# Linear attention's level stage with one mixed array of queries and keys, a fourth product bank, and a reordered start, in a four-layer network on one core

## The reference, cut to what matters

```python
def first_block(...):        # layers 0 and 1
    for i in range(2):
        u = modulate(h, shift, scale)
        y = attention_mixer(u) if i == 0 else ssm_mixer(u)
        h = layer_norm(ALPHA * h + g_m * y, ...)
        f = squared_relu_mlp(modulate(h, ...), ff_w1[i], ff_w2[i])   # 1024 -> 4096 -> 1024
        h = layer_norm(ALPHA * h + g_f * f, ...)

def second_block(...):       # layers 2 and 3
    for i in range(2):
        a = rms_norm(h) * (1 + scale) + shift
        o = even_mix(a) if i == 0 else attention(a)
        h = h + gate * o
        h = h + gate2 * conv_ffn(rms_norm(h) * (1 + scale2) + shift2)
    return rms_norm(h_lat, g_norm_final)

def even_mix(h, ...):        # layer 2: Fourier mixing beside gated linear attention
    u_f, q, k, v, r, z = split(h @ w_in)
    loga = log_sigmoid(z @ w_gate + b_gate) / 16       # a decay per key channel and token
    o = gla_scan(q, k, v, loga forwards) + flip(gla_scan(flipped))
    # within a chunk: A[i, j] = sum_c q[i,c] k[j,c] exp(sum of loga between j and i),  j <= i
```

## Time and profile before

| | |
|---|---|
| device time, median of 3 runs | 4260.65 us (4259.33 to 4261.77) |
| profiled execution | 4259.32 us, span 4257.5 us |
| busy in the span | PE 4039.0 us (95%), DVE 1786.7 (42%), ACT 815.5 (19%), POOL 240.6 (6%) |
| mean granted clock | 0.980 of full |
| first 28 us | DMA busy share 0.96, 359 GB/s |
| level stage, 2573.6 to 2769.5 us | 195.90 us: PE 141.57 busy, DVE 150.75, ACT 71.11, POOL 0.00; granted clock 0.78 |
| pairs of layer 2, 2896.2 to 3273.7 us | 377.50 us: PE 371.00 busy, DVE 278.43 |
| pairs of layer 3, 3824.5 to 4098.2 us | 273.70 us: PE 264.90 busy, DVE 220.83 |

### The profile page before, as it was taken

One profiled execution on the slowest core, in us unless ns is written; L12 is line 12 of the kernel. 1 busy time (PEld: TensorE's weight loads), 2 busy tenths in 40 slices (PEclk: granted clock), 3 DMA queues, 4 the chain that ended last, 5 costly groups with the idle time before them and its releaser, 6 DMA issues.

```text
span 4257.5 us, 45853 instructions
## 1 busy us (share of the span) xinstructions
PE 4039.0 (95%) x18528; PEld 2498.0 (59%) x18528; DVE 1786.7 (42%) x3040; ACT 815.5 (19%) x1549; POOL 240.6 (6%) x228
## 2 busy tenths in 40 slices
PE   7999999999999999999999996799999999999999
PEld 5676588744455555558646545645555444758864
DVE  0254523100266655444102028736776015437841
ACT  1265111100112321111102022321100021531000
POOL 1000000000013441300000000000000000000000
PEclk9999999999999999999999997799999999999999
DMA  4255011211112211322223012301111112002222
GB/s 179 90 198 180 20 60 60 70 59 43 41 68 101 90 65 64 120 73 84 95 74 113 35 42 100 139 21 60 54 56 60 54 66 70 2 21 89 80 89 74
DMA packets 201230, 325.82 MB, mean 77 GB/s; under 512 B 4274, under 2 KB 90616, under 8 KB 200896
## 3 DMA queue, kind: packets, MB, share of 16 engines
q1 hardware_dynamic: 195136, 302.00, 20.6%
q0 software_dynamic: 5888, 20.91, 1.5%
HBM read 320.74 MB, written 2.16 MB: 76 GB/s over the span
## 4 chain that ended last, share of the span: by engine, by line
PE 88%; DVE 7%; ACT 3%; issue 1%; DMA 1%; POOL 0%; DVEq 0%; ACTq 0%; SPq 0%
PE PS L973 27%; PE PS L1013 22%; PE PS L948 3%; PE PS L1485 3%; PE PS L926 3%; PE PS L1064 3%; PE PS L1499 3%; PE PS L885 2%; PE PS L805 2%; PE PS L1486 1%; PE PS L1646 1%; PE PS L1178 1%; PE PS L1656 1%; PE PS L1337 1%; PE PS L1147 1%
## 5 line engine op out<-in xcount | busy, mean ns | idle before, releaser
L973 PE MATMUL PS<-RING,BIG 128*128 128x512 f32 x2352 | 1016.9, 593 | 3.7 <-DVEq L1713 1.6
L973 PEld LDWEIGHTS PS<-RING,BIG 128*128 128x128 f32 x2352 | 445.5, 190 | 557.1 <-issue 552.2
L1013 PE MATMUL PS<-UT,RING 128*128 128x256 f32 (+1 forms) x2432 | 648.2, 414 | 35.1 <-ACT BIG L2510 18.3
L1013 PEld LDWEIGHTS PS<-UT,RING 128*128 128x128 f32 x2432 | 461.3, 191 | 188.5 <-issue 25.3
L1013 PE MATMUL PS<-BIG,RING 128*128 128x256 f32 (+1 forms) x1824 | 487.6, 410 | 1.5 <-DVEq L1733 1.0
L1800 DVE TENSOR_TENSOR RES_TMP<-PS,GATE 128x512 f32<-128x512 f32 x80 | 55.3, 692 | 1030.2 <-PE PS L973 960.0
L1013 PEld LDWEIGHTS PS<-BIG,RING 128*128 128x128 f32 x1824 | 346.1, 190 | 107.1 <-DVEq L1733 3.1
L948 PE MATMUL PS<-RING,UT 128*128 128x512 f32 x320 | 141.1, 603 | 2.5 <-ACT BIG L2784 0.9
L973 PE MATMUL PS<-RING,UT 128*128 128x512 f32 x320 | 139.2, 593 | 2.0 <-issue 1.2
L1485 PE MATMUL PS<-UT,RING 128*128 128x512 f32 x256 | 132.4, 599 | 3.8 <-issue 3.1
L2493 ACT ACTIVATE UT<-PS,COL 128x128 f32<-128x128 f32 x328 | 119.1, 468 | 75.6 <-PE PS L863 73.3
(11 more groups left out here) (403 smaller groups left out, 4686.3 us busy)
## 6 DMA issues: line engine op xcount, KB each, us to landing
RING<-w_mod_dram SPq DMA_DIRECT2D x48, 2048.0 KB, 8.0
RING<-w_ffn_up_dram SPq DMA_DIRECT2D x44, 1024.0 KB, 5.0
RING<-ff_w_dram SPq DMA_DIRECT2D x32, 1024.0 KB, 5.4
RING<-ff_w_dram SPq DMA_DIRECT2D x16, 2048.0 KB, 7.8
RING<-ssm_w_in_dram SPq DMA_DIRECT2D x8, 2048.0 KB, 7.8
RING<-w_ffn_down_dram SPq DMA_DIRECT2D x8, 1536.0 KB, 6.6
RING<-w_ffn_down_dram SPq DMA_DIRECT2D x8, 1280.0 KB, 5.7
RING<-ssm_w_out_dram SPq DMA_DIRECT2D x4, 2048.0 KB, 7.8
```

Source lines behind the costliest of these rows:

```text
L973: m = mm(bank(t), inp[:, kk, t * 128:(t + 1) * 128], w[:, k, :], start=kk == 0, stop=kk == kn - 1)
L1013: m = mm(bank(bank_, n), a[:, k, :], b[:, k, :], start=k == 0, stop=k == 3)
```

## The change

It has four parts.

1. **Level stage.** A level needs q only in one half of each stretch and k only in the other, so one array C_MIXED holds for every level q's half and k's half. GpSimd lays it together (`mixed_halves`): per round 14 copies of 128 elements for each partition. VectorE's `products` is one multiplication of 1792 columns in place of two, and waits for these copies. TensorE uses the one array for both operands. The copies under a mask touch half the columns for levels 0 to 6. Level 7, which uses raw q and k, comes first, ahead of the wait for the product. The mask table is smaller.
2. **Start.** The context tokens' DMA goes behind the arrival of the latent tokens and the bias, the attention constants behind three used weight tiles. Tiles 0 and 1 are transposed inside the modulation, and the first tile's second 256 columns are done as 128 and 128.
3. **Banks.** Product 3 gets a bank of its own (bd: 6 or 7) in layers 1 to 3, and waits for no take; product 1 of pair p+2 waits for take 3. In layer 0 the banks stay.
4. **Boundaries.** In layers 0 and 1, ScalarE's turned(t-1) stands ahead of root(t).

```diff
@@ product_banks
-            return ((0, 2, 3), (1, 4, 5))[p % 2] if tiles_of(L)[0] == NT else ((4, 0, 1), (5, 2, 3))[p % 2]
+            if L == 0:
+                return ((0, 2, 3, 0), (1, 4, 5, 1))[p % 2]
+            return ((0, 2, 3, 6), (1, 4, 5, 7))[p % 2] if L == 2 else ((4, 0, 1, 6), (5, 2, 3, 7))[p % 2]
@@ modulation_start
+                    if L == 0 and m == 2:
+                        turn_tokens(0, "m", 0, "tokens_turned", 0)
+                        turn_tokens(0, "m", 1, "tokens_turned_too", 2)
@@ paired_up on TensorE: one, seven_three_four
-                        pe.wait_ge(S("quarters_taken"), 7 * (n0 + p - 2) + 5)
+                        pe.wait_ge(S("quarters_taken"), 7 * (n0 + p - 2) + (3 if L else 5))
...
                     done(product(bb, s3, t3))
-                    pe.wait_ge(S("quarters_taken"), 7 * (n0 + p) + 3)
-                    done(product(ba, s4, b22))
+                    if L == 0:
+                        pe.wait_ge(S("quarters_taken"), 7 * (n0 + p) + 3)
+                    elif p < 2:
+                        seen(L, "f", ntok - 1)
+                    done(product(bd, s4, b22))
@@ mixer0 on TensorE
-                for t in range(TL):
-                    turn_tokens(0, "m", t, *(("tokens_turned", 6), ("tokens_turned_too", 4))[t % 2])
+                turn_tokens(0, "m", 2, "tokens_turned", 4)
+                turn_tokens(0, "m", 3, "tokens_turned_too", 6)
...
-                early_tile(0, "m", t0, f, None, 2, [(0, 256, 2), (256, 256, 3)], [(LAT, 128, 4), (LAT + 128, 128, 5)], {(0, 1): context})
+                seen(0, "m", 0)
+                early_tile(0, "m", t0, f, None, 2, [(0, 256, 1), (256, 128, 2), (384, 128, 3)], [(LAT, 128, 4), (LAT + 128, 128, 5)], {(0, 2): context})
@@ levels on TensorE
-                        pe.wait_ge(S("L2_levels_ready"), 2 * t + dr + 1)
-                        for v_ in range(GLA_LEVELS):
+                        for v_ in LEVEL_ORDER:
+                            if v_ == 0:
+                                pe.wait_ge(S("L2_levels_ready"), 2 * t + dr + 1)
...
-                                kk = C_KL[rows, v_, a, :] if v_ < 7 else C_QK[rows, 2 + a, ts]
-                                qq = C_QL[rows, v_, a, :] if v_ < 7 else C_QK[rows, a, ts]
+                                kk = C_ML[rows, v_, a, :] if v_ < 7 else C_QK[rows, 2 + a, ts]
+                                qq = C_ML[rows, v_, a, :] if v_ < 7 else C_QK[rows, a, ts]
@@ products on VectorE
-                    for dst, a in ((C_QL, 0), (C_KL, 2)):
-                        step(V.tensor_tensor(dst, C_EXP, C_QK[:, a:a + 2, ts].unsqueeze(1).to_broadcast([128, 7, 2, 128]), ALU.mult))
+                    dve.wait_ge(S("L2_halves_mixed"), 14 * (n + 1))
+                    step(V.tensor_tensor(C_ML, C_EXP, C_MIXED, ALU.mult))
@@ masked copies on VectorE
-                        b = (n * GLA_LEVELS + v_) % 2 * 2
+                        data = PS[:, i % 2 * 1024:i % 2 * 1024 + 1024].rearrange("p (s x) -> p s x", s=2)[:, :, 0:256]
...
+                            give(lv, V.copy_predicated(halves_of(at, v_, 1 - dr), level_mask(dr, v_), halves_of(data, v_, 1 - dr)))
@@ takes on VectorE
-                    take(V.tensor_tensor(q12, q22, bank(ba, n), ALU.add))
+                    take(V.tensor_tensor(q12, q22, bank(bd, n), ALU.add))
@@ boundaries on ScalarE
                     for t in range(ntok):
-                        if L >= 2:
-                            if t:
-                                turned_(t - 1)
-                            rms(L, "f", t, "m_residual_ready", tiles_before(L, "f"))
-                            continue
-                        root(L, which, t)
                         if t:
                             turned_(t - 1)
+                        if L < 2:
+                            root(L, which, t)
+                        else:
+                            rms(L, "f", t, "m_residual_ready", tiles_before(L, "f"))
@@ GpSimd
-            bring("tokens_in", H[:, TL:NT, :], d["ctx"][0].rearrange("(t p) n -> p t n", p=128))
+            pool.wait_ge(S("tokens_in"), 16)
+            def mixed_halves():
+
+                for n in range(2 * NT):
+                    t, dr = n // 2, n % 2
+                    if n:
+                        pool.wait_ge(S("L2_levels_ready"), n)
+                    q, k = (C_QK[:, a:a + 2, t * 128:(t + 1) * 128] for a in (0, 2))
+                    for v_ in range(7):
+                        for src, h in ((q, 1 - dr), (k, dr)):
+                            nc.gpsimd.tensor_copy(halves_of(C_MIXED[:, v_], v_, h), halves_of(src, v_, h)).then_inc(S("L2_halves_mixed"), 1)
...
             bring_bias(layers[0])
+            bring("tokens_in", H[:, TL:NT, :], d["ctx"][0].rearrange("(t p) n -> p t n", p=128))
...
+                    pool.wait_ge(wused, 3)
                     bring("attention_constants_in", A_CONST, d["c_att"])
...
+                    mixed_halves()
```

82 lines of the change are left out of this document (46 added, 36 removed).

## The result

| | before | with the change |
|---|---|---|
| median of four runs | 4259.99 us (4255.01 to 4261.77) | 4209.04 us (4206.36 to 4216.12) |
| profiled execution | 4259.32 us, span 4257.5 | 4210.7 us, span 4208.9 |
| TensorE, busy | 4039.0 us (95%) | 4021.7 us (96%) |
| mean granted clock | 0.980 | 0.983 |

The ratio is 0.9885 (interval 0.9868 to 0.9902): faster by some 50 us, where 32 were forecast. The direction and the sign of every part were right; the sum was 16 us short. (In rows, PE is TensorE, DVE VectorE, ACT ScalarE, POOL GpSimd and SP SyncE.)

The account below looks back on a forecast made before the run. TensorE, at work 95% of the span, was taken as the bound. Start 2.3, boundaries 3.7, banks 20.2 and level stage 6.0 sum to 32.2 us off 4259.3, so 4227.1, as median 4228; range 4213 to 4243.

Parts of the forecast that it names:

- 16.4: Level stage: us saved by the single product, half masks and level 7 first, before any charge for GpSimd's copies.
- 10.4: Level stage: us charged for GpSimd's copies holding up VectorE, 40 operations at 0.26 each.
- lower bound of 0.13: Level stage: least us one GpSimd copy holds up a VectorE operation, half of 0.26 for one input rather than two.
- the slack: Level stage, after odd rounds: ScalarE's exponentials end only 0.9 us before the next product, so savings there count 1.8 us.
- another circle takes over: Layer 3's pairs: VectorE's take 2 to take 7, then the next product 6, limits a pair to 12.34 us; gain 6.0.
- upper bound of 23: Fourth bank, layers 2 and 3 together: most us it could save; the forecast was 20.2, the lower bound 12.
- the seven other waits of this layer: Layer 3: TensorE's waits beside the ten of 0.58 us, put at 4.8 us, of which 2.9 were counted as gain.
- the DMA term: Start: context and attention constants leave the way of the first weights; 0 to 2 us, taken as 1.0.
- (a): Level stage: copies are cheap or don't meet the differences; stage gives 11 to 16 us, time 4216 to 4223; chance 0.20.
- (b): Level stage: copies are dear, 0.4 to 0.9 us each; stage gives 0 to -20, time 4234 to 4254; chance 0.17.
- (c): Fourth bank: the wait moves to other products because VectorE is the pace; 8 to 12 us less gain, 4236 to 4240; chance 0.12.
- (d): Level stage: GpSimd itself becomes the pace, with copies of 1.04 us; slower, 4269 us; chance 0.04.

Follow-up runs that it names:

- number 6: The changed kernel, but GpSimd's copies of a round wait until VectorE's seven differences are done; 4205.37 us, ratio 0.9876.
- number 7: The changed kernel with each GpSimd copy replaced by an addition of the same 128 elements to themselves; one run, 4217.2 us.
- experiment 8: The changed kernel with one GpSimd copy of 1792 elements a round in place of fourteen of 128; one run, 4203.49 us.
- experiment 9: The kernel before with only half masks and level 7 first, still two products and no GpSimd; 4248.86 us, ratio 0.9977.
- experiment 5: The changed kernel, but GpSimd lays together the array for the first round only, and the other eleven rounds reuse it; 4206.09 us, ratio 0.9877.

## Why the prediction was right or wrong

**The level stage, by 12 of the 16 us.** The forecast was 16.4 - 10.4 = 6.0; it gave 18.1. Two steps failed: the charge for the copies was 6.4 too high, and the 16.4 was 5.7 too low.

The first: "So each difference is charged one copy, x. A quarter of 1044 is 0.26 for 128 elements." The timeline of the changed kernel, one round odd and one even:

```profile
2630.55 2.02 DVE L2041 TENSOR_TENSOR UT<-UT 128x1792 f32<-128x1792 f32 x1 [1.63 <-ACTq L2471]
...
2632.70 5.19 POOL L3074 COPY UT<-BIG 128x128 f32<-128x128 f32 x14 [9.93 <-DVEq L1756]
...
2633.66 0.82 DVE L2094 TENSOR_TENSOR GB<-GB,BIG 128x512 f32<-128x512 f32 x1
...
2634.62 3.11 DVE L2034 TENSOR_TENSOR UT<-BIG 128x256 f32<-128x256 f32 x7
...
2646.18 2.02 DVE L2041 TENSOR_TENSOR UT<-UT 128x1792 f32<-128x1792 f32 x1 [0.21 <-DVE GB L2111]
...
2648.32 4.72 POOL L3074 COPY UT<-BIG 128x128 f32<-128x128 f32 x14 [10.43 <-DVEq L1756]
...
2659.21 1.70 ACT L2764 ACTIVATE UT<-UT 128x1792 f32<-128x1792 f32 x1
...
2660.98 2.02 DVE L2041 TENSOR_TENSOR UT<-UT 128x1792 f32<-128x1792 f32 x1 [1.63 <-ACTq L2471]
```

and its groups of differences and copies, which answer to the earlier trace rows:

```profile
L2034 DVE TENSOR_TENSOR UT<-BIG x84: 414/504/543, 2536.0 to 2710.4; 128x256 f32<-128x256 f32 x84
L3074 POOL COPY UT<-BIG x168: 283/298/752, 2533.1 to 2712.2; 128x128 f32<-128x128 f32 x168
```

GpSimd's copy lasts 298 ns (297 in number 6, where it meets no difference), so its length was nearly right, and the mechanism too: seven differences take 3.11 rather than 2.44, the heads' operation 0.82 rather than 0.69. But of these 298 ns only the 0.1 by elements hold VectorE up. The charge was 40 times 0.26, and measured 5 x (0.67 + 0.13) = 4.0. The row used had 512 elements with two inputs. Of the excess of 0.17 for an operation, the larger part is the second input: the addition of 128 elements in number 7 holds up by 0.196, the copy of one input by 0.085. The lower bound of 0.13, "one input rather than two, half", was the better value. The forecast said of its choice that "width must tell": it does, but the inputs tell as much. The Trainium skill's "SBUF — State Buffer", Who interferes with whom, says that the port pair is held for a whole instruction; the 1510 of 1680 ns of experiment 8 nearly agree with it, and the 85 of 298 of the short copy do not: a whole copy for each of the forty operations would have cost 12 us (an estimate, 40 times 0.298), where 4.0 were measured. The measurement decides.

The second: "In the odd round's copies nothing is saved, for TensorE's levels at the low clock pace them", and "only what lies within this slack counts ... 1.8". The low clock was taken as given, and what follows the last product was given no more than its part of the queue. The stage as a whole, from the first product to the output projection, with the change:

```profile
2552.02:2742.71 190.69, 139.08 (x1812) 116.52 (x1813) 126.58 (x221) 71.08 (x117) 52.26 (x154) 0.84 0.38 133
```

The granted clock is 0.84 where the stage had 0.78, and TensorE is busy for 139.08 us with the work that took 147.86. The half masks, which the sum valued at no more than the 1.8 of the slack, brought 8.1 alone in the profiled execution (experiment 9), with the clock of the even rounds at 0.98 to 1.00. Of the slack the step was right in kind: an even round ends by ScalarE's exponentials (2659.21 + 1.70, then the product at 2660.98). The five of them took 13.7 to 16.6 before and 13.9 to 14.8 now, 2.95 less in sum against the 1.8. The five odd rounds are 7.8 less, where the queue with the measured hold-up gives 6.2. The largest surplus is at the two ends, ahead of the second product and behind the last: 7.35 less (2.69 and 4.66), where the sum had 4.4 (two products and 0.3). Behind the last product, 24 matmuls of the levels take 2.04 where they took 3.35, and the granted clock is 0.80 where it was 0.71. The three surpluses, 1.15, 1.6 and 2.95, are the 5.7.

The 16.4 for the stage without contention was low as well: experiment 5, in which there is none, gained 25.6. That the clock moves so much with a few tenths of a microsecond on VectorE is shown, and that TensorE stood still for less ahead of the faster matmuls; what exactly raises or lowers it is not shown, and no experiment changed the clock by itself.

**Banks: 20.2 forecast, 22.9 in the pairs, 1.0 of it given back.** Layer 2's 11.9 was 12.0, layer 1's nothing was nothing. In layer 3 the step "another circle takes over ... after which the next product 6 may start: 12.34" failed. The timeline of a pair of layer 3 with the change:

```profile
3977.87 0.42 DVE L2412 TENSOR_TENSOR BIG<-BIG,PS 128x256 f32<-128x256 f32 x1
...
3978.07 1.89 PE L1031 MATMUL PS<-BIG,RING 128*128 128x256 f32 x8
...
3981.20 0.42 DVE L2396 TENSOR_TENSOR BIG<-BIG,PS 128x256 f32<-128x256 f32 x1
...
3981.80 0.42 DVE L2398 TENSOR_TENSOR BIG<-BIG,PS 128x256 f32<-128x256 f32 x1 [0.17 <-PE PS L1031]
...
3983.25 1.89 PE L1031 MATMUL PS<-BIG,RING 128*128 128x256 f32 x8
```

Take 7 ends at 3978.29, and product 6 of the next pair had started at 3978.07: it does not wait for this take 7. In the program (`six_and_five`) product 6 of pair p waits for `7 * (n0 + p - 1)` takes, that is for take 7 of pair p-2, a whole period earlier, since two pairs alternate between two sets of banks. The forecast had joined two ends that are neighbours in time, though the wait between them points one pair further back. What binds is TensorE alone, with 12.10 for a pair; VectorE waits 0.17 ahead of take 2, for product 5. So the upper bound of 23 was nearly the value. The term for "the seven other waits of this layer" was misread, too: of the 17 waits and 10.6 us, five with 2.9 us lie in layer 2, and two with some 1.9 were left for layer 3 beside the ten of 0.58. By the periods alone ten pairs give 8.7 of the 10.9.

**Start: 2.3 forecast, 3 to 4 measured.** The mechanism held in part; the DMA term (1.0 of 0 to 2) came out at 1.5, from 37.16 to 35.62. Unforeseen is that the last tile's matmuls run at the full clock, 1.95 where they took 3.23: before, TensorE had stood still for 3.48 us ahead of them, and now it transposes there. That is 1.3 of the 3.5 by which ScalarE starts earlier, so the nearness of the sum is partly luck. **Boundaries: 3.7 forecast, 3.6 measured** in TensorE's waits, by the steps as written: of the 2.90, 1.1 were lost to the later root.

**Rivals.** (a) was right about the copies (0.1 for an operation) and too small, since it took over the same 16.4. (b), (c) and (d) did not come; (d)'s price rested on a copy of 1.04 us. The upper bounds of all four parts together made 49.7 (4.5 + 5.8 + 23 + 16.4), and the kernel gained 48.6 by its trace; but the range's low end took those of start and boundaries only, and the stage went past its own bound of 16.4.

## What to carry to other kernels

GpSimd work beside VectorE operations with two SBUF inputs cost VectorE here about the element part of each GpSimd instruction that an operation met, once for each operation: 0.1 us from a short copy, 1.5 from a long one. Better than either was to let the copies start when VectorE turned to operands in PSUM, which took one more wait and gave some 4 us more. Before a wait in time is called a circle, look for the semaphore that closes it, and for the round that it counts: here it pointed one pair further back. In a stage with a lowered TensorE clock the clock is no constant of the estimate, and the mean of the stage says too little: what counted was whether the lower clock fell on the matmuls for which the next engine waits.
